# Banded grouped-query attention: heads in pairs on TensorE instead of one by one

## The reference

```python
SWA_HEADS, SWA_KV_HEADS, SWA_HEAD_DIM, SWA_WINDOW = 32, 4, 64, 128   # 8 heads share one key/value head
qkv = h @ w_qkv
scores = einsum('bnqkgd,bnskd->bnkgqs', q, kb) * 64 ** -0.5           # block of 128 queries, band of 256 keys
scores = where(mask, scores - slope[head] * dist, -1e30)
probs = softmax(concat([scores, sink[head]]))[..., :-1]
out = einsum('bnkgqs,bnskd->bnqkgd', probs, vb)
h = h + out.reshape(B, S, 2048) @ w_o
```

## Time and profile before

| | |
|---|---|
| median of 3 runs | 2471.1 us (2470.93 to 2472.24) |
| span of the profiled execution, first to last instruction | 2468.7 us |
| busy, share of the span | TensorE matmul 98%, weight load 96%, VectorE 66%, ScalarE 46% |
| attention of layer 1 in it | from 170.27 to about 386.04 us: 215.8 us, 8.7% of the span |

### The profile page before, as it was taken

The page is one execution under the profiler, slowest core; times in us unless marked ns, Lnnn a source line. Parts: engine busy times, 40 slices in busy tenths (PEclk is TensorE's granted clock), DMA queues, the critical chain, the costliest instruction groups (busy, mean ns, idle before and its releaser), DMA issues.

```text
span 2468.7 us, 45014 instructions
## 1 busy us (share of the span) xinstructions
PE 2425.4 (98%) x19390; PEld 2362.2 (96%) x19390; DVE 1638.5 (66%) x1808; ACT 1140.8 (46%) x1274; POOL 8.6 (0%) x19
## 2 busy tenths in 40 slices
PE   6999999999999999999999999999999999999998
PEld 6898889999999999999999989889999999999998
DVE  5766677766666656665756866887656666666655
ACT  5545445644434434444535444556444444434444
POOL 1000000000000000000000000000000000000000
PEclk9999999999999999999999999999999999999999
DMA  7653433455555555555564454445555555555552
GB/s 262 200 170 119 136 103 139 169 188 187 181 178 185 186 177 181 187 170 189 170 205 154 158 174 163 154 137 172 182 192 177 180 187 176 183 185 187 178 180 69
DMA packets 211819, 423.93 MB, mean 172 GB/s; under 512 B 6896, under 2 KB 7184, under 8 KB 211216
## 3 DMA queue, kind: packets, MB, share of 16 engines
q1 hardware_dynamic: 211152, 421.69, 50.8%
q0 software_dynamic: 576, 0.92, 0.3%
HBM read 420.48 MB, written 2.10 MB: 171 GB/s over the span
## 4 chain that ended last, share of the span: by engine, by line
PE 96%; DVE 2%; ACT 1%; DMA 1%; issue 0%; SPq 0%; DVEq 0%; ACTq 0%
PE pair L307 31%; PE pair L309 30%; PE pair L308 30%; PE pair L609 1%; DVE wlo L221 1%; PE pair L600 0%; PE pair L620 0%; PE pair L599 0%; DMA raw<-in_x_w_kv 0%; ACT whi L213 0%; DMA raw<-in_mem 0%; PE pair L621 0%; PE pair L622 0%; PE pair L524 0%; PE pair L862 0%
## 5 line engine op out<-in xcount | busy, mean ns | idle before, releaser
L221 DVE TENSOR_TENSOR wlo<-raw,whi 128x2048 fp32r<-128x2048 f32 x396 | 905.7, 2290 | 488.7 <-ACT whi L213 488.5
L213 ACT ACTIVATE whi<-raw 128x2048 fp32r<-128x2048 f32 x396 | 756.4, 1912 | 974.3 <-PE pair L309 967.1
L307 PE MATMUL pair<-xhi,whi 128*128 128x256 f32 x4128 | 1175.9, 285 | 10.3 <-DVE wlo L221 9.0
L309 PE MATMUL pair<-xhi,wlo 128*128 128x256 f32 x4128 | 1169.1, 283 | 0.0
L308 PE MATMUL pair<-xlo,whi 128*128 128x256 f32 x4128 | 1169.1, 283 | 0.0
L307 PEld LDWEIGHTS pair<-xhi,whi 128*128 128x128 f32 x4128 | 793.3, 192 | 20.7 <-issue 19.0
L308 PEld LDWEIGHTS pair<-xlo,whi 128*128 128x128 f32 x4128 | 793.4, 192 | 1.2 <-issue 1.0
L309 PEld LDWEIGHTS pair<-xhi,wlo 128*128 128x128 f32 x4128 | 793.2, 192 | 0.0
L307 PE MATMUL pair<-ohi,whi 128*128 128x256 f32 x1792 | 510.0, 285 | 1.0 <-DVE olo L1476 1.0
L309 PE MATMUL pair<-ohi,wlo 128*128 128x256 f32 x1792 | 507.1, 283 | 0.0
L308 PE MATMUL pair<-olo,whi 128*128 128x256 f32 x1792 | 507.1, 283 | 0.0
(11 more groups left out here) (184 smaller groups left out, 1186.5 us busy)
## 6 DMA issues: line engine op xcount, KB each, us to landing
raw<-in_ffn_w_up SPq DMA_DIRECT2D x176, 1024.0 KB, 5.0
raw<-in_ffn_w_down SPq DMA_DIRECT2D x88, 1024.0 KB, 5.0
raw<-in_diff_w_qkv SPq DMA_DIRECT2D x48, 1024.0 KB, 5.1
raw<-in_swa_w_qkv SPq DMA_DIRECT2D x20, 1024.0 KB, 5.1
raw<-in_x_w_kv SPq DMA_DIRECT2D x16, 1024.0 KB, 6.3
raw<-in_swa_w_o SPq DMA_DIRECT2D x16, 1024.0 KB, 5.0
raw<-in_diff_w_o SPq DMA_DIRECT2D x16, 1024.0 KB, 5.1
raw<-in_x_w_q SPq DMA_DIRECT2D x8, 1024.0 KB, 5.5
```

Of the source, the lines that this page charges most:

```text
L213: act.activation(whi[:, s], raw[:, s], ACT.Copy).then_inc(hi_ready, 1)
L221: dve.tensor_tensor(wlo[:, s], raw[:, s], whi[:, s].bitcast(F32), ALU.subtract)\
L307: pe.matmul(dst, ahi, bhi, start=start, stop=False, skip_group_check=True)
L309: return pe.matmul(dst, alo, bhi, start=False, stop=stop, skip_group_check=True)
```

## The change

On TensorE the loop over 8 heads becomes a loop over 4 pairs. The scores of a pair's two heads are issued together: both heads' first matmul, one in each half of the array's rows, and then both heads' second. The value products of a pair are issued together too, three times two, one in each half of the array's columns. The pair's scores now wait for both heads of the pair before to be biased, and the value products for the copies of both heads. The units and the transposes are placed anew between them. VectorE, ScalarE, SP and their orders stay as they are, and so does every number that is computed.

```diff
-            def swa_scores(g, j):
...
-                if not isinstance(g, int) or 8 * g + j >= 2:
-                    pe.wait_ge(swa["biased"], g * 8 + j - 1)
...
+            def swa_scores(g, p):
...
+                if not isinstance(g, int) or 4 * g + p >= 1:
+                    pe.wait_ge(swa["biased"], g * 8 + 2 * p)
+                halves = [slice(64 * i, 64 * i + 64) for i in range(2)]
+                for i, half in enumerate(halves):
+                    pe.matmul(PC[:, 512 * i:512 * i + P], q_sb[half, p, Q0], swa_kg[half, 0:P],
+                              start=True, stop=True)
+                for i, half in enumerate(halves):
+                    pe.matmul(PC[:, 512 * i + P:512 * i + 3 * P], q_sb[half, p, Q1], swa_kg[half, :],
+                              start=True, stop=True).then_inc(swa["scores"], 1)
...
+            def swa_pv(g, p):
+
+                pe.wait_ge(swa["pT_evac"], g * 8 + 2 * p + 2)
+                if not isinstance(g, int) or 4 * g + p >= 1:
+                    pe.wait_ge(swa["o_evac"], g * 4 + p)
+                halves = [slice(64 * i, 64 * i + 64) for i in range(2)]
+                for i, half in enumerate(halves):
+                    pe.matmul(pv_ps[half, 0:P], swa_vg[:, 0], ptbuf[:, i, 0:P], start=True, stop=True)
+                for i, half in enumerate(halves):
+                    pe.matmul(pv_ps[half, P:2 * P], swa_vg[:, 0], ptbuf[:, i, P:2 * P], start=True, stop=False)
+                for i, half in enumerate(halves):
+                    pe.matmul(pv_ps[half, P:2 * P], swa_vg[:, 1], ptbuf[:, i, 2 * P:3 * P],
+                              start=False, stop=True).then_inc(swa["pv"], 1)
...
-                for j in range(8):
-                    swa_scores(g, j)
-                    if j % 2 == (0 if with_o else 1) and with_q:
-                        if j < 2:
+                for p in range(4):
+                    swa_scores(g, p)
+                    if p >= 2:
+                        swa_pv(g, p - 2)
+                    if p >= 1:
+                        turn_probs(swa, g, 8, 2 * p - 2, pbuf[:, 0], THREE)
+                    if with_q:
+                        if p == 0:
                             pe.wait_ge(swa["q_evac"], g * 2 + 2)
-                        proj_unit(pe, b4, j if with_o else j // 2, PA, xhi, xlo, j // 2, j < 2, j >= 6)\
+                        proj_unit(pe, b4, 2 * p if with_o else p, PA, xhi, xlo, p, p == 0, p == 3)\
                             .then_inc(units_used, 1)
-                    if j % 2 == 1 and with_o:
-                        o_unit(swa, g, b4, j if with_q else j // 2, j // 2, with_q)
-                    if j >= 1:
-                        turn_probs(swa, g, 8, j - 1, pbuf[:, (j - 1) % 2], THREE)
-                    if j >= 2:
-                        swa_pv(g, j - 2)
+                    else:
+                        o_unit(swa, g, b4, p, p, with_q)
+                    if p >= 1:
+                        turn_probs(swa, g, 8, 2 * p - 1, pbuf[:, 1], THREE)
+                    if with_q and with_o:
+                        o_unit(swa, g, b4, 2 * p + 1, p, with_q)
+                swa_pv(g, 2)
+                turn_probs(swa, g, 8, 6, pbuf[:, 0], THREE)
                 if with_q:
                     turn_probs(swa, g, 8, 7, pbuf[:, 1], THREE)
-                    swa_pv(g, 6)
-                    swa_pv(g, 7)
+                    swa_pv(g, 3)
...
             last_part(swa, B_SWA + 8, 0, 0)
             turn_probs(swa, 3, 8, 7, pbuf[:, 1], THREE)
-            swa_pv(3, 6)
             last_part(swa, B_SWA + 8, 1, 0)
-            swa_pv(3, 7)
+            swa_pv(3, 3)
```

More of the change, by code:

```diff
@@ L588, in _ @@
                     turn_rstd(pe, R_MIX[0])
-            def swa_scores(g, j):
-                if j % 4 == 0:
-                    pe.wait_ge(swa["q_evac"], g * 2 + j // 4 + 1)
-                if j == 0:
+            def swa_scores(g, p):
+                if p % 2 == 0:
+                    pe.wait_ge(swa["q_evac"], g * 2 + p // 2 + 1)
+                if p == 0:
                     pe.wait_ge(swa["group_ready"], g + 1)
-                if not isinstance(g, int) or 8 * g + j >= 2:
-                    pe.wait_ge(swa["biased"], g * 8 + j - 1)
[L597 to L601, removed]
+                if not isinstance(g, int) or 4 * g + p >= 1:
[7 more added lines that the diff above has]
+                              start=True, stop=True).then_inc(swa["scores"], 1)
             def turn_probs(s, g, per, j, src, blocks):
```

## The result

The changed kernel takes **2459.13 us** (median of 4 runs, 2457.71 to 2460.50), the kernel before 2471.67 us beside it: a ratio of 0.9948, 95% interval 0.9934 to 0.9962. It is 12.5 us faster. The forecast was 2454.1 us with a range of 2451.5 to 2459.5 us; the time lies 0.4 us inside the range's slow edge.

What follows compares the result with a forecast made beforehand. TensorE, 96% of the span, was taken as the bound. Groups 1 and 2 -11.8, group 0 -3.7, group 3 -1.5: -17.0 us from 2468.7, plus 2.4 for the median, gives 2454.1 us; 8-in-10 range 2451.5 to 2459.5.

Steps and rivals of the forecast that it cites:

- The halves run side by side: Attention pairs on TensorE: two heads' scores take 0.86 us together, two heads' value products 0.81 us.
- Groups 1 and 2: Layer-1 attention, middle groups: -6.46 us up to the last unit, +0.57 us behind it, net -5.9 us a group.
- Group 0: First attention group: -6.7 us up to the last unit, +3.1 us at its end, net -3.7 us.
- group 3: Last attention group: -5.2 us before its end, +3.7 us at its end, net -1.5 us.
- The dear ends: Ends of groups 0 and 3, with odd transposes behind the last unit: +3.1 and +3.7 us.
- the 5.8 us ahead of the quarter block: Group 3's end: from head 5's transposes, ScalarE and VectorE work up to `o_lo_half` delays the first quarter block 5.8 us.
- The sum: All four attention groups together: -17.0 us, with everything later untouched.
- the clock falls in a new wait: Rival, 4%: TensorE drops to half clock at group 3's end, costing some 4.5 us: 2459 us, or 2463 if at both ends.
- 3.5 us is well under 8.7: Argument against the clock falling: group 3's new wait is shorter than the early 20.00 to 28.70 us without matmuls.
- The forecast's own case: The laid-out sum without any rival, 77%: 2452.5 us (end waits half as long) to 2456.5 us (five waits 0.5 us longer).
- rivals at 2459 us: Program order on TensorE, clock falling in a new wait, VectorE or ScalarE holding TensorE more often; together 13%.
- program order holds on TensorE: Rival, 4%: matmuls start and end as written, costing score pairs 0.22 and value pairs 0.11 us more, +5.3 us, 2459 us.

Runs made afterwards that it cites:

- with the clock held: The changed kernel plus throwaway matmuls on TensorE in its two longest waits, at the ends of groups 0 and 3: 2455.70 us, ratio to before 0.9939.
- the kernel with early transposes: The changed kernel, but in groups 0 and 3 a pair's two transposes stand before the unit again: 2450.43 us, ratio to before 0.9914.

## Why the prediction was right, and what was off

*The halves run side by side*: right. A pair takes 0.86 and 0.80 us, and taking the halves away costs 0.65 us for each pair.

*Groups 1 and 2*, forecast -5.9 us each: with the clock held, 58.63 us a group for 58.4 forecast, -5.7 us each.

*Group 0*, forecast -3.7, and *group 3*, forecast -1.5: with the clock held, 39.2 and 43.4 us for 38.9 and 43.1, so -3.4 and -1.2 us. The dear ends and the 5.8 us ahead of the quarter block are there; from odd transposes to scores it is 1.36 us (182.65 to 184.01 in the changed kernel) and 1.27 us (191.80 to 193.07), where 1.2 were laid out. As the changed kernel runs, group 0 has 40.0 us and group 3 45.8, which is longer than before.

*The sum*: 17.0 us forecast, 16.0 us in the profile with the clock held, 11.14 in the changed kernel's. The step that failed is in the rival "the clock falls in a new wait", at 4%: "3.5 us is well under 8.7". I took the length of the only such wait in the trace as a bound for a wait that is still safe. It was none, and the trace of the kernel before already says so. TensorE's last matmul ahead of that wait ends at 19.77 us, and two stretches of it are:

```profile
20.00:25.00 5.00, 0.00 (x0) 0.00 (x0) 0.00 (x0) 0.66 (x1) 0.00 (x0) 0.89 1.05 256
25.00:30.00 5.00, 1.28 (x6) 1.31 (x7) 3.72 (x5) 3.94 (x7) 0.00 (x0) 0.50 0.97 367
```

From 1.00 to 0.50 a mean of 0.89 puts the fall at about 23.9 us, some 4.1 us after the last matmul and not 8.7. In the changed kernel it came still sooner: in both of its profiles the clock fell behind or in the waits of 1.9 and 3.4 us at the ends of groups 0 and 3, and once also behind shorter ones. The rival's price of 4.5 us for one place was too high: 2.4 and 2.5 us measured, since the clock stayed down for 6.8 us and not 10, and TensorE waited in a part of that anyway. With both places it comes to 4.9 us, near the 2459 us it named for one.

That the time still lies in the range is in part luck. The forecast's own case, 2452.5 to 2456.5 us, holds for the kernel with the clock held (2455.70 us) and not for the changed kernel. The slow edge of 2459.5 us stands where it does because of rivals at 2459 us, and the one that came true had 4%. The second measurement of the same kernel, 2459.91 us, lies outside.

*The order*: I put "program order holds on TensorE" at 5.3 us and 4%. In the order as written nothing is lost (0.80 us a value pair). But the reason given, that four passes of one line start ahead of the next line, does not carry to value products: written head by head they lose 0.28 us a pair. The interleaving in the change is worth that. The Trainium skill's rule (page "TensorE: Matmul & The Clock Gate", section on packing small matmuls) that matmuls start in program order fits neither row: the second head's scores start ahead of the first's third and fourth pass, and its values, written head by head, ahead of the first's last three.

## What to carry to other kernels

Two heads with a dimension of 64 cost TensorE no more than one here, if their products lie in different halves and are written alternately. Before moving an instruction behind a long block, follow the chain that its result starts: here an odd head's transposes start some 4 us of VectorE and ScalarE work, and with them behind the last unit, groups 0 and 3 gave back most of what pairs had saved. Read the granted clock around every new wait on TensorE, price what follows the wait at half clock too, and put real work there if you can.

## What was not expected of the hardware

- Throwaway matmuls in two waits made the kernel 3.4 us faster (2455.70 against 2459.13 us), with the clock at 1.00 instead of 0.79 and 0.73 over the ends of groups 0 and 3.
- Written head by head, a value pair takes 1.08 us instead of 0.80, while a score pair stays at 0.86 us.
- With one row half for both heads the clock also fell behind group ends whose single waits are 0.7 to 0.9 us, once in the kernel with early transposes (0.52 over 266.45 to 270.00 us there), and once in the second profile of the changed kernel. In other profiles with the same waits it did not. What decides it stays open.
